# Bringing one expert's rows back with a weighted one-hot product instead of a store and a gather, in a two-layer hybrid decoder

## What is computed

```python
def _moe(h, router, w1, w3, w2):
    logits = jnp.einsum('btd,de->bte', h, router).astype(jnp.float32)
    top_v, top_i = lax.top_k(logits, TOP_K)            # TOP_K = 2
    gates = jax.nn.softmax(top_v, axis=-1)
    combine = jnp.einsum('btk,btke->bte', gates,
                         jax.nn.one_hot(top_i, N_EXP, dtype=jnp.float32)).astype(h.dtype)
    y = jnp.zeros_like(h)
    for e in range(N_EXP):                             # N_EXP = 8, D_EXP = 3584
        y = y + combine[..., e:e + 1] * _swiglu(h, w1[e], w3[e], w2[e])
    return y
...
        h = _rmsnorm(x, W['ln_ffn'][l])
...
            x = x + _moe(h, W['moe_router'][l // 2], W['moe_w1'][l // 2], W['moe_w3'][l // 2], W['moe_w2'][l // 2])
...
    y = _rmsnorm(x, W['ln_final'])
```

## Time and profile before

| | |
|---|---|
| median of 3 runs | 1897.18 us (1895.52 to 1899.0) |
| the profiled execution's own time | 1901.34 us |
| its span, first to last instruction | 1899.5 us |
| PE busy | 1811.1 us, 95% of the span |
| DVE, ACT, POOL busy | 468.4, 243.5, 92.1 us |
| mean granted PE clock | 0.958 of full speed |
| eight experts | 994.3 to 1868.3 us of the span |
| after PE's last product | 1868.3 to 1899.5 us |

### The profile page before, as it was taken

The page is one execution under the profiler, slowest core; times in us unless marked ns, Lnnn a source line. Parts: engine busy times, 40 slices in busy tenths (PEclk is TensorE's granted clock), DMA queues, the critical chain, the costliest instruction groups (busy, mean ns, idle before and its releaser), DMA issues.

```text
span 1899.5 us, 38385 instructions
## 1 busy us (share of the span) xinstructions
PE 1811.1 (95%) x17692; PEld 986.6 (52%) x17692; DVE 468.4 (25%) x1021; ACT 243.5 (13%) x558; POOL 92.1 (5%) x121
## 2 busy tenths in 40 slices
PE   7999899999999999989989999999999999999993
PEld 5778876666665677878562333333333333333330
DVE  2435654300001243664441001001000101000112
ACT  1342222100000134221210000000000000000000
POOL 0000012100000000001210000000000000000000
PEclk9999997999999899988769999999999999999997
DMA  7330011733320323001189999999999999999981
GB/s 235 106 104 3 3 65 64 297 123 140 134 102 2 128 100 104 3 3 65 64 340 390 402 401 414 404 420 416 407 419 405 419 400 415 419 411 416 413 346 60
DMA packets 66808, 454.02 MB, mean 239 GB/s; under 512 B 10256, under 2 KB 37200, under 8 KB 42192
## 3 DMA queue, kind: packets, MB, share of 16 engines
q1 hardware_dynamic: 60704, 431.43, 56.7%
q0 software_dynamic: 5520, 19.89, 2.8%
q10 hardware_dynamic: 416, 0.16, 0.0%
HBM read 441.47 MB, written 9.99 MB: 238 GB/s over the span
## 4 chain that ended last, share of the span: by engine, by line
PE 92%; DVE 5%; ACT 1%; issue 1%; DMA 1%; POOL 0%; DVEq 0%; SPq 0%; ACTq 0%; POOLq 0%
PE bank L529 90%; PE bank L533 2%; DVE ring L1328 1%; DVE work L1328 1%; DVE work L1331 1%; DVE hT L1328 0%; DMA work<-y_rows,token_row 0%; ACT work L2113 0%; DMA X<-x_in_dram 0%; DVE X L1328 0%; DVE X L2081 0%; DVE AV L1654 0%; ACT ring L2098 0%; ACT ring L2182 0%; DVE hT L1722 0%
## 5 line engine op out<-in xcount | busy, mean ns | idle before, releaser
L529 PE MATMUL bank<-ring,hT 128*32 128x512 f32 (+2 forms) x6336 | 625.5, 538 | 0.7 <-DVE hT L1328 0.7
L529 PEld LDWEIGHTS bank<-ring,hT 128*32 128x32 f32 (+1 forms) x6336 | 223.5, 112 | 401.5 <-issue 387.9
L529 PE MATMUL bank<-hT,ring 128*128 128x288 f32 x1632 | 410.8, 412 | 1.6 <-DVEq L1372 1.6
L529 PE MATMUL bank<-ring,work 128*32 128x512 f32 (+4 forms) x3168 | 390.4, 569 | 0.0
L529 PEld LDWEIGHTS bank<-hT,ring 128*128 128x128 f32 x1632 | 312.6, 193 | 100.6 <-issue 13.8
L1328 DVE TENSOR_TENSOR work<-work,bank 128x384 f32<-128x384 f32 (+2 forms) x142 | 77.9, 560 | 768.5 <-ACT work L2325 504.6
L529 PEld LDWEIGHTS bank<-ring,work 128*32 128x32 f32 (+3 forms) x3168 | 129.7, 116 | 238.6 <-issue 235.5
L2325 ACT ACTIVATE work<-bank 128x512 f32<-128x512 f32 (+1 forms) x48 | 26.1, 544 | 569.0 <-PE bank L529 569.0
L529 PE MATMUL bank<-ring 64*64 64x64 f32 (+11 forms) x1152 | 79.4, 288 | 5.3 <-DVE SS L1328 2.7
L2098 ACT ACTIVATE ring<-bank 128x32 f32<-128x32 f32 (+7 forms) x144 | 41.3, 335 | 196.3 <-PE bank L529 172.4
L529 PEld LDWEIGHTS bank<-ring 64*64 64x64 f32 (+6 forms) x1152 | 55.9, 148 | 20.1 <-issue 13.1
(11 more groups left out here) (235 smaller groups left out, 1005.8 us busy)
## 6 DMA issues: line engine op xcount, KB each, us to landing
ring<-moe_dram SPq DMA_DIRECT2D x168, 2048.0 KB, 10.8
ring<-ffn_dram SPq DMA_DIRECT2D x22, 1536.0 KB, 12.9
ring<-w_in_dram SPq DMA_DIRECT2D x18, 1536.0 KB, 6.5
ring<-w_out_dram SPq DMA_DIRECT2D x2, 1536.0 KB, 6.9
work<-w_out_dram SPq DMA_DIRECT2D x2, 1280.0 KB, 8.3
ring<-w_out_dram SPq DMA_DIRECT2D x2, 1280.0 KB, 10.1
ring<-w_in_dram SPq DMA_DIRECT2D x2, 1152.0 KB, 5.3
C<-consts_dram SPq DMA_DIRECT2D x1, 1912.5 KB, 13.3
```

What stands on the lines that cost most here:

```text
L529: return nc.tensor.matmul(out, lhsT, rhs, start=start, stop=stop, skip_group_check=True)
```

## The change

The last expert's rows no longer go through HBM. A one-hot matrix `picks` (slots of expert 7 against rows, each entry the row's gate) is built by DVE right after the slot lists, in the order of the 128 rows of banks 6 and 7, doubled group included. PE turns it during the last expert's `down_pair` (6 transposes), ACT copies it to `picks_t`. After the last `down_pair`, PE multiplies it with `y_exp` (6 products, banks 0 to 5), and DVE adds the products to `X` (`add_tail`). The gather of the higher numbered expert's rows out of `y_rows` runs during expert 7, with the weight set to zero where that expert is number 7 (`row_weight` column 4). The sums of squares and the roots of the final norm stand ahead of the branch. The tiles come in the order 2, 0, 1.

```diff
@@ PE: expert(r, e)
                     if p == 2 and e < N_EXP - 1:
                         turn(job + 1)
+                    if p == 2 and job == LAST:
+                        turn_picks()
+                if job == LAST:
+                    tail()
+
+            def turn_picks():
+                pe.wait_ge(picks_ok, 1)
+                pe.wait_ge(up_ok, 6 * N_EXP)
+                for c in range(2):
+                    for t, (t0, n) in enumerate(TILES):
+                        i = tr(pe, banks[3 + c][:, t0:t0 + n], picks[0:n, t, c, :])
+                    i.then_inc(picks_full, 1)
+
+            def tail():
+                pe.wait_ge(picks_in, 2)
+                pe.wait_ge(y_first, N_EXP)
+                pe.wait_ge(y_ready, 3 * LAST + 1)
+                for t in TAIL_ORDER:
+                    t0, n = TILES[t]
+                    for c in range(2):
+                        mm(pe, banks[2 * t + c][0:n, :], picks_t[c][:, t0:t0 + n], y_exp[:, c * 512:(c + 1) * 512])\
+                            .then_inc(tail_full, 1)
@@ DVE
+            def last_picks():
+
+                for t, (t0, n) in enumerate(TILES):
+                    w = route[0:n, 1, t, LAST:LAST + 1]
+                    for c, parts in enumerate((((0, 0, CAP), (CAP, 0, GROUP)), ((0, 0, 2 * GROUP), (2 * GROUP, GROUP, CAP)))):
+                        for at, s0, s1 in parts:
+                            i = V.tensor_scalar(picks[0:n, t, c, at:at + s1 - s0], hot[0:n, t, LAST, s0:s1], w, None, MUL)
...
+                own(V.tensor_scalar(small[:, 4, :, 0], first[:, :, 1], LAST * CAP - 0.5, None, ALU.is_lt))
+                settle()
+                own(tt(row_weight[:, :, 4], row_weight[:, :, 1], small[:, 4, :, 0], MUL))
+                own(V.tensor_scalar(first, first, LAST * CAP - 1.0, None, ALU.min))
...
                 if r == 0:
+                    last_picks()
                     token_rows()
@@ DVE: output_in(job)
                 V.tensor_copy(y_exp[:, 512:], banks[Y_BANKS[1]][:, :]).then_inc(y_ready, 1)
+                if job == LAST:
+                    for _ in range(2):
+                        V.engine_nop().then_inc(y_ready, 1)
+                    return
@@ DVE: expert(r, e), last_outputs(r)
                 gated(job, 1)
+                if job == LAST:
+                    add_back(2, 4)
...
                 if r == 0:
-                    add_back(2, 1)
+                    add_tail()
+            def add_tail():
+                for at, t in enumerate(TAIL_ORDER):
+                    n = TILES[t][1]
+                    for c in range(2):
+                        dve.wait_ge(tail_full, 2 * at + c + 1)
+                        x = X[0:n, t, c * 512:(c + 1) * 512]
+                        own(tt(x, x, banks[2 * t + c][0:n, :], ADD))
+                    settle()
+                    V.engine_nop().then_inc(tail_added, 1)
+                    square_sum(t, n, fss_ok)
@@ ACT
+            def last_outputs(r):
+                output_in(r * N_EXP + LAST)
+                if r == 0:
+                    for at, t in enumerate(TAIL_ORDER):
+                        root(t, (fss_ok, 0, at), frs_ok)
@@ POOL: expert(r, e), last_of_round(r)
                     gather_back(1, 0)
-                store_outputs(job, e, r)
+                    gather_back(2, 1)
+                else:
+                    store_outputs(job, e, r)
...
-                    pool.wait_ge(y_saved, 48 * N_EXP)
-                    gather_back(2, 1)
```

More of the change, by code:

```diff
@@ L339, in trunk @@
         token_row = ctx.enter_context(nc.sbuf_tensor("token_row", [P, 3, 4], mybir.dt.int32))
-        row_weight = sb("row_weight", 3, 4)
+        row_weight = sb("row_weight", 3, 5)
+        picks = g2[:, :, :].rearrange("p a b -> p (a b)").rearrange("p (t c s) -> p t c s", t=3, c=2)
+        picks_t = [x[:, :, :].rearrange("p a b -> p (a b)")[:, 0:NT] for x in (U1, AV)]
         hn_rows = nc.dram_tensor("hn_rows", [NT, D], F32).ap()
@@ L490, in trunk @@
         turned = counter("expert_rows_transposed")
+        picks_ok = counter("last_expert_picks_ready")
+        picks_full = counter("last_expert_picks_turned")
+        picks_in = counter("last_expert_picks_copied")
+        tail_full = counter("last_expert_rows_ready")
+        tail_added = counter("last_expert_rows_added")
+        late_squares = counter("late_squares_summed")
+        late_roots = counter("late_rstd_ready")
         y_first = counter("expert_output_first_half_copied")
@@ L596, in trunk @@
         Y_BANKS = (6, 7)
+        LAST = N_EXP - 1
+        TAIL_ORDER = (2, 0, 1)
+        saved = lambda job: 48 * (job - 1 if job > LAST else job)
         DOWN_ROUNDS = (((0, 0), (0, 0), (0, 0), (0, 1)), ((1, 0), (0, 1), (0, 1), (1, 0)), ((1, 1), (1, 0), (1, 1), (1, 1)))
@@ L1328, in tt, with row_squares @@
                 return V.tensor_tensor(out, a, b, op)
+            def row_squares(t, n):
+                return V.tensor_tensor_reduce(junk[0:n], X[0:n, t, :], X[0:n, t, :], 1.0, 0.0, MUL, ADD, stat[0:n, t, 0:1])
             def square_sum(t, n, done):
-                own(V.tensor_tensor_reduce(junk[0:n], X[0:n, t, :], X[0:n, t, :], 1.0, 0.0, MUL, ADD, stat[0:n, t, 0:1]))
+                own(row_squares(t, n))
                 settle()
@@ L1888, in list_slots @@
                 listed(1, banks[4], 1, N_EXP)
+            def last_picks():
[4 more added lines that the diff above has]
+                            i = V.tensor_scalar(picks[0:n, t, c, at:at + s1 - s0], hot[0:n, t, LAST, s0:s1], w, None, MUL)
+                            if (t, c, at) != (2, 1, 2 * GROUP):
+                                own(i)
+                settle()
+                i.then_inc(picks_ok, 1)
             def token_rows():
@@ L2072, in _ @@
             dve.wait_ge(lnf_in, 16)
[L2073 to L2082, removed]
+            for at, t in enumerate(TAIL_ORDER):
+                n = TILES[t][1]
+                wait(dve, frs_ok, 0, at)
+                own(V.reciprocal(stat[0:n, t, 2:3], stat[0:n, t, 1:2]))
+                settle()
+                V.scalar_tensor_tensor(X[0:n, t, :], X[0:n, t, :], stat[0:n, t, 2:3], lnf[0:n, :], MUL, MUL)\
+                    .then_inc(final_ok.sem, 1)
         @block.scalar
@@ L2098, in copy, with root_of, late_root @@
                 return A(out, in_, ACT.Copy)
+            def root_of(t):
+                n = TILES[t][1]
+                return A(stat[0:n, t, 1:2], stat[0:n, t, 0:1], ACT.Sqrt, bias=eps(0)[0:n], scale=1.0 / D)
+            def late_root(t):
+                root_of(t).then_inc(late_roots, 1)
             def root(t, summed, done):
-                n = TILES[t][1]
                 wait(act, *summed)
-                A(stat[0:n, t, 1:2], stat[0:n, t, 0:1], ACT.Sqrt, bias=eps(0)[0:n], scale=1.0 / D).then_inc(done.sem, 1)
+                root_of(t).then_inc(done.sem, 1)
             def norm(l, use):
@@ L2329, in output_in @@
                 if job:
-                    act.wait_ge(y_saved, 48 * job)
+                    act.wait_ge(y_saved, saved(job))
+                if job == N_EXP:
+                    act.wait_ge(tail_full, 6)
                 copy(y_exp[:, 0:512], banks[Y_BANKS[0]][:, :]).then_inc(y_first, 1)
@@ L2338, in expert @@
                 expert_silu(job, 1)
+                if job == LAST:
+                    for c in range(2):
+                        act.wait_ge(picks_full, c + 1)
+                        copy(picks_t[c], banks[3 + c][:, 0:NT]).then_inc(picks_in, 1)
+            def last_outputs(r):
+                output_in(r * N_EXP + LAST)
+                if r == 0:
+                    for at, t in enumerate(TAIL_ORDER):
+                        root(t, (fss_ok, 0, at), frs_ok)
+                if r == ROUNDS - 1:
+                    for at, t in enumerate(TAIL_ORDER):
+                        act.wait_ge(late_squares, at + 1)
+                        late_root(t)
             act.dma_start(C[:, 0:P], consts[:, 0:P]).then_inc(first_inputs, 16)
@@ L2402, in _ @@
                     routing(l)
-                    expert_rounds(act, expert, last=lambda r: output_in(r * N_EXP + N_EXP - 1))
-            for t in range(3):
-                root(t, (fss_ok, 0, t), frs_ok)
+                    expert_rounds(act, expert, last=last_outputs)
         @block.sync
@@ L2480, in _ @@
                         load_expert(r, e)
-            for t, (t0, n) in enumerate(TILES):
-                wait(sp, final_ok, 0, t)
+            for at, t in enumerate(TAIL_ORDER):
+                t0, n = TILES[t]
+                wait(sp, final_ok, 0, at)
                 sp.dma_start(y_out[t0:t0 + n, :], X[0:n, t, :]).then_inc(y_stored, 16)
@@ L2567, in gather_back @@
                     pool.wait_ge(back_added, 3 * (turn - 1))
-                src = y_rows[0][0:(N_EXP - 1) * CAP] if which == 0 else y_rows[which // 2]
+                src = y_rows[1] if which // 2 else y_rows[0][0:LAST * CAP]
                 for t, (t0, n) in enumerate(TILES):
```

17 lines of the change are left out of this document (13 added, 4 removed).

## The result

| | kernel before | changed kernel |
|---|---|---|
| median of the runs | 1899.04 us (12 runs, 1895.52 to 1908.66) | 1892.51 us (12 runs, 1889.64 to 1898.99) |
| ratio | | 0.9964, 95% interval 0.9950 to 0.9978 |
| span of the profiled execution | 1899.5 us | 1887.9 us |

The change made the kernel faster, by 6.8 us of 1899 (4.2 to 9.5). The forecast was 8.6 less and a time of 1888.6, with a range of 1885.3 to 1891.6. The span of the profiled executions fell by 11.6, more than either number.

What follows compares the result with a forecast made beforehand. PE, busy 95% of the span, was taken to bound the kernel, followed by a serial end of 31.2 us. The new end summed to 22.6, 8.6 less; from the median 1897.18 that gave 1888.6 us, range 1885.3 to 1891.6.

Steps and rivals of the forecast that it cites:

- what bounds the end: After PE's last product, 31.2 us in which PE does nothing and each step waits for the one before it.
- six transposes count in whole: In the last `down_pair` PE is full, so the six transposes of the picks add 0.8 us.
- DVE paces the tail from the second tile on: Tail adds and squares: PE's products are ahead, so DVE sets the pace, 2.75 us for each of tiles 0 and 1.
- the picks, the gather and its adds are hidden: Picks built in DVE's idle time before expert 0's gating, second gather and adds within expert 7: no added time.
- the clock stays up: PE's tail products run at clock 1.00 despite the 0.8 us idle before them, about 0.9 us each.
- the branch keeps its stall: DVE's branch before the final multiplications still jumps and takes 3.9 us as before, 2.92 of it unnamed.
- the first three: Rivals: branch loses its stall, 1885.3, chance 0.05; clock falls in tail, 1891.6, chance 0.1; weights come late, 1901, chance 0.02.
- the fourth, an end that moves less than counted: Rival: waits between engines add some 0.5 us for each of six steps, 3 us and more, 1892; chance 0.08.
- their 20 us of lead: Weight blocks in expert 7 land 20 us early, so the 2 us the second gather delays them costs nothing.
- The last store: At the end, now 512 KB instead of 128 KB: 3.2 us instead of 2.6.
- The copy and PE's answer: After PE's last w2 product, DVE's copy of `y_exp` and PE's start on the tail: 0.8 us.
- the rest of the tail: Tile 2's products and add 1.1 + 0.9 + 0.7, squares and other tiles 1.4 + 5.5, final multiplications 4.25 us.

Runs made afterwards that it cites:

- the second measurement: The changed kernel, unchanged, run again against the kernel before: ratio 0.9975 (0.9962 to 0.9988), a gain of 4.7 us.
- the second traces: Both kernels profiled again without edit: kernel before against itself 1.0012, span 1894.9 us, end stretch 30.4; changed kernel's ratio 0.9975, end stretch 22.3.

## Why the forecast's gain was near and its time was not

**Right.** The forecast had right what bounds the end, that six transposes count in whole, that DVE paces the tail from the second tile on, that the picks, the gather and its adds are hidden, that the clock stays up, and that the branch keeps its stall. Of the rivals the first three did not come, and of the fourth, an end that moves less than counted, a third: 1.0 of its 3 us. The clock was 1.00 through the tail; the weights lost 3.5 to 3.7 of their 20 us of lead, where 2.1 was counted, and it cost nothing; DVE's stall was 3.17 and 3.05 instead of going.

**Off in size.** The sum said 31.2 - 22.6 = 8.6. The runs show:

- The old end is 31.2 in one trace and 30.4 in the next, by the landing of a gather and of the stores. One trace stood for both: 0.4 too much on the mean.
- The transposes were put at 0.8, from eight of 128 rows in a row, with the two narrow ones counted as cheaper. The six took 1.2; each three (128, 128 and 32 rows) took 0.55, the narrow one no less than the others. Why is open: the eight of 96 rows in expert 6, also among products, took 0.88.
- The branch was put at 3.9. From the end of the last sum it took 1875.84 to 1880.05, 4.2.
- The last store was put at 3.2. From 1884.29 to 1887.9 it is 3.6.
- The copy and PE's answer took 0.9 instead of 0.8; the rest of the tail was 0.1 to 0.2 less than counted.

New: 22.4 + 1.2 = 23.6 instead of 22.6. Old: 30.8. The change is worth 7.2 by the traces, which lies within 4.2 to 9.5 and at the upper end of the second measurement's 2.3 to 7.2. The mean of the two measurements is 5.8, 1.4 less; with such a spread the runs are too few to say whether the traces leave something out.

**Wrong.** The time was missed by 3.9: 1.9 by the level from which the gain was taken, 1.4 by the terms above, and 0.7 that no run explains and that is less than the runs' spread. The step that failed most is the last one: "I take the difference from the median: 1897.18 - 8.6 = 1888.6", with "the runs' own spread of 1.8 around their median" inside the range. The median of three runs was taken for the level of the kernel. Twelve runs had it at 1899.04, and the 35 beside the second traces at 1899.64. The spread is 12 to 13 us, not 3.5; the first twelve runs, taken by threes, have medians of 1897.18, 1901.06, 1899.05 and 1899.72. With 1899.04 and 7.2 the sum is 1891.8; 1892.51 was measured, and 1894.72 the second time. Had either error alone been made, the range, moved along, would just have held the result (up to 1893.5 or 1893.0); it had room for one thing going wrong at a time, not for several together. The profile had shown a warning: its own execution took 1901.34, outside the three runs, and the clock fell and rose at several places ahead of the experts. I looked at the clock in the tail only, where it did nothing, and not in the stages where it differs from one execution to the next. A range that took in an uncertain level would have been wider by some 2 to 3 us on both sides, an estimate from these four medians.

**Open.** Which stretches get half the clock in an execution was seen, not steered, so that this causes the whole spread of the times is argued from two traces and the clocks of the runs. The slow first products of one trace do not show in its granted clock. The landmark in expert 6 lay between 1726.7 and 1731.5 in the twelve traces of this study, whatever the kernel.

## What to carry to other kernels

Where the matrix engine is idle at the end, a round trip through HBM (store, landing, gather, landing) can be replaced by a product with a one-hot matrix that is built and turned while other engines wait; here six products and their adds took the place of 13.5 us of copy, folds, stores and gathers, at a price of 1.2 us of transposes. Put a branch that jumps far where its engine waits anyway, not between the last data and the result. When a change is worth a few tenths of a percent, read the start of its stage as a landmark in both traces, and do not forecast an absolute time from three runs of a kernel whose clock moves.

## What the hardware showed that was not expected

- One program on one core, unchanged, varied by 12 us (0.65%) in 35 executions, along with its mean granted clock (0.953 to 0.963).
- In one of two traces of the same program PE's first products, from 17.5 us on, took 714 ns each instead of 406, for some 3 us, with a granted clock of 1.00 in the table for both.
- DVE's jump over the further rounds costs 2.85 to 3.17 us beyond reading and comparing; a jump over nothing costs 0.16. Two packets of the instruction queue came within the wait, and none at the jump over nothing.
- Three gathers of 1.2 MB in all, beside a full weight stream, made the median weight block land 3.5 us later; beside an earlier gather of the same size it was 2.1.
- Six transposes, four of 128-row and two of 32-row tiles by turns, took 0.2 us each on the mean, where eight of 128 rows in a row took 0.14 each.
